# Two stacked transformer blocks on one core: the odd attention's probabilities scaled on GpSimd, the second turned tile taken by VectorE one step behind

## What is computed

```python
def window_attention(q, k, v, k_c, v_c, sink):       # 16 query heads, 4 key heads of 64
    s_loc = jnp.einsum('bkgnqd,bkncd->bkgnqc', qb, kb) * scale      # latent keys, |i-j| <= 128
    s_loc = jnp.where(valid, s_loc, -jnp.inf)
    s_ctx = jnp.einsum('bkgnqd,bkld->bkgnql', qb, k_c) * scale      # 256 context keys
    m = jnp.maximum(jnp.maximum(jnp.max(s_loc, -1, keepdims=True), jnp.max(s_ctx, -1, keepdims=True)), s_sink)
    e_loc = jnp.exp(s_loc - m)
    e_ctx = jnp.exp(s_ctx - m)
    denom = jnp.sum(e_loc, -1, keepdims=True) + jnp.sum(e_ctx, -1, keepdims=True) + jnp.exp(s_sink - m)
    o = (jnp.einsum('bkgnqc,bkncd->bkgnqd', e_loc, vb)
         + jnp.einsum('bkgnqc,bkld->bkgnqd', e_ctx, v_c)) / denom
```

## Time and profile before

| | |
|---|---|
| time, median of 3 runs | 2239.7 us (2237.48 to 2242.08) |
| the profiled execution | 2240.83 us, its span 2239.0 us |
| busy in the span | PE 97%, DVE 80%, ACT 53%, POOL 5% |
| odd attention in the span | about 1946 to 2006 us |
| TensorE's granted clock, mean | 0.992 of full speed |

### The profile page before, as it was taken

How to read it: one execution, slowest core, us unless ns; L and a number is a source line. 1 busy time by engine, 2 the same in 40 slices (tenths; PEclk the granted TensorE clock), 3 DMA queues, 4 the chain that set the end, 5 groups by cost and what they waited for, 6 DMA issues and landing times.

```text
span 2239.0 us, 34046 instructions
## 1 busy us (share of the span) xinstructions
PE 2162.9 (97%) x14088; PEld 1885.2 (84%) x14088; DVE 1796.2 (80%) x2404; ACT 1184.7 (53%) x1785; POOL 109.9 (5%) x157
## 2 busy tenths in 40 slices
PE   7999999999999999999999999999999999999997
PEld 4888889888878889898888978878888888767886
DVE  4988787788888878878888777779798988787764
ACT  3554556555455445655544545437646744485742
POOL 1000000000000000000000000000000000000000
PEclk9999999999999999999999999999999999999999
DMA  9889665488858868556887717528778877404662
GB/s 333 283 278 325 220 221 197 151 268 278 300 194 278 303 209 294 174 186 209 277 309 243 263 27 246 202 68 290 266 279 268 298 260 254 132 5 153 218 209 76
DMA packets 330881, 506.28 MB, mean 226 GB/s; under 512 B 12375, under 2 KB 239926, under 8 KB 330727
## 3 DMA queue, kind: packets, MB, share of 16 engines
q1 hardware_dynamic: 288503, 341.75, 46.1%
q0 software_dynamic: 41616, 160.44, 20.6%
q10 hardware_dynamic: 608, 1.92, 0.3%
HBM read 503.03 MB, written 1.05 MB: 225 GB/s over the span
## 4 chain that ended last, share of the span: by engine, by line
PE 78%; DVE 14%; DMA 3%; ACT 3%; issue 1%; POOL 0%; DVEq 0%; ACTq 0%; POOLq 0%
PE banks L617 35%; PE banks L618 18%; PE banks L609 6%; PE banks L611 5%; PE banks L610 5%; DVE wlo L1874 3%; PE banks L801 1%; DMA plain_xs<-in_ada_w_dram 1%; DVE arena L1899 1%; PE banks L862 1%; DVE nraw L2146 1%; DMA modw<-in_w_mod_dram 1%; DMA stage<-in_ffn_wg_dram 1%; DVE plain_hs L1899 1%; DVE xs L2150 1%
## 5 line engine op out<-in xcount | busy, mean ns | idle before, releaser
L1874 DVE TENSOR_TENSOR wlo<-stage,whi 128x1024 fp32r<-128x1024 f32 x644 | 757.9, 1219 | 136.1 <-ACT whi L1378 135.0
L1378 ACT CAST whi<-stage 128x1024 fp32r<-128x1024 f32 x644 | 643.9, 1051 | 351.6 <-PE banks L618 265.7
L617 PE MATMUL banks<-xs,whi 128*128 128x512 f32 x2176 | 766.4, 397 | 15.0 <-DVE xs L2150 9.5
L618 PE MATMUL banks<-xs,wlo 128*128 128x256 f32 x2176 | 608.7, 280 | 0.0
L617 PEld LDWEIGHTS banks<-xs,whi 128*128 128x128 f32 x2176 | 408.8, 188 | 116.5 <-DVE xs L2150 9.4
L618 PEld LDWEIGHTS banks<-xs,wlo 128*128 128x128 f32 x2176 | 411.1, 189 | 0.0
L609 PE MATMUL banks<-xs,whi 128*128 128x256 f32 x1216 | 352.1, 290 | 15.0 <-DVE xs L2072 7.9
L617 PE MATMUL banks<-hidden_arena,whi 128*128 128x512 f32 x992 | 354.6, 399 | 0.2 <-DVE wlo L1874 0.2
L610 PE MATMUL banks<-xs,whi 128*128 128x256 f32 x1216 | 344.6, 283 | 0.0
L611 PE MATMUL banks<-xs,wlo 128*128 128x256 f32 x1216 | 344.5, 283 | 0.0
L618 PE MATMUL banks<-hidden_arena,wlo 128*128 128x256 f32 x992 | 278.8, 281 | 0.0
(11 more groups left out here) (414 smaller groups left out, 2716.8 us busy)
## 6 DMA issues: line engine op xcount, KB each, us to landing
stage<-in_mlp_w_dram SPq DMA_DIRECT2D x96, 1024.0 KB, 5.5
modw<-in_w_mod_dram POOLq DMA_DIRECT2D x80, 1024.0 KB, 5.9
modw<-in_ada_w_dram POOLq DMA_DIRECT2D x66, 1024.0 KB, 5.5
stage<-in_ffn_wg_dram SPq DMA_DIRECT2D x44, 1024.0 KB, 5.5
stage<-in_ffn_wu_dram SPq DMA_DIRECT2D x44, 1024.0 KB, 7.3
stage<-in_ffn_wd_dram SPq DMA_DIRECT2D x44, 1024.0 KB, 7.2
stage<-in_ev_w_in_dram SPq DMA_DIRECT2D x24, 1024.0 KB, 6.5
stage<-in_w_in_dram SPq DMA_DIRECT2D x18, 1024.0 KB, 5.3
```

The lines of the kernel that those rows point to most:

```text
L617: mm(out, hi, pair.rearrange("p a t -> p (a t)"), start=first_mm, stop=False, skip_group_check=True)
L618: return mm(out[:, 0:T], lo, pair[:, 0, :], start=False, stop=last_mm, skip_group_check=True)
L1378: nc.scalar.copy(halves(whi[:, s, :], n, h, True), halves(stage[:, s, :], n, h)).then_inc(hi_done, 1)
L1874: last = v.tensor_tensor(halves(wlo[:, s, :], n, h, True), halves(stage[:, s, :], n, h), halves(whi[:, s, :], n, h, True).bitcast(F32), AL ...
```

## The change

DVE's `normalise(s)` stops after the reciprocal and signals `odshare` with a small memset. POOL scales the two tiles, all 16 steps of it ahead of the last modulation vector's transfers in its queue, and PE's `turn(s)` waits for POOL. ACT's `take(s)` copies the first turned tile only. DVE copies the second in `take_second(s-1)`, behind `normalise(s)`. The waits follow: `exps(s)` for the turn of step s-2, the reciprocal for POOL's step s-2 (its column is reused), `values(s)` and `turn(s)` for both takers.

```diff
+        pool_out = signal("pool_out")
...
+            def normalise(s):
+                o = 20 * (s % 2)
+                pool.wait_ge(dve_out.sem, dve_out.at(("odshare", s)))
+                for e in range(2):
+                    p = ODD["p"][s % 2][:, e, :]
+                    last = nc.gpsimd.tensor_scalar(p, p, stat[:, o + 12 + e:o + 13 + e], None, ALU.mult)
+                last.then_inc(pool_out.sem, pool_out.next(("odprob", s)))
             for m in range(NMOD):
+                if m == NMOD - 1:
+                    for s in range(16):
+                        normalise(s)
...
                 def turn(s):
-                    pe.wait_ge(dve_out.sem, dve_out.at(("odprob", s)))
+                    pe.wait_ge(pool_out.sem, pool_out.at(("odprob", s)))
                     for e in range(2):
                         if s >= 1:
-                            pe.wait_ge(drained.sem, drained.at(("odpt", s - 1, e)))
+                            taker = drained_v if e else drained
+                            pe.wait_ge(taker.sem, taker.at(("odpt", s - 1, e)))
...
                 def values(s):
-                    pe.wait_ge(drained.sem, drained.at(("odpt", s, 1)))
+                    pe.wait_ge(drained.sem, drained.at(("odpt", s, 0)))
+                    pe.wait_ge(drained_v.sem, drained_v.at(("odpt", s, 1)))
...
                 def exps(s):
+                    if s >= 2:
+                        act.wait_ge(pe_out.sem, pe_out.at(("odpt", s - 2, 1)))
...
                 def take(s):
-                    for e in range(2):
-                        act.wait_ge(pe_out.sem, pe_out.at(("odpt", s, e)))
-                        if s >= 2 and e == 0:
-                            act.wait_ge(pe_out.sem, pe_out.at(("odpv", s - 2)))
-                        nc.scalar.copy(O["pt"][s % 2][:, :, e * P:(e + 1) * P], Y[:, 2 + e, :].rearrange("p (a q) -> p a q", a=4)) \
-                            .then_inc(drained.sem, drained.next(("odpt", s, e)))
+                    act.wait_ge(pe_out.sem, pe_out.at(("odpt", s, 0)))
+                    if s >= 2:
+                        act.wait_ge(pe_out.sem, pe_out.at(("odpv", s - 2)))
+                    nc.scalar.copy(O["pt"][s % 2][:, :, 0:P], Y[:, 2, :].rearrange("p (a q) -> p a q", a=4)) \
+                        .then_inc(drained.sem, drained.next(("odpt", s, 0)))
...
                     link(v.tensor_tensor(stat[:, o + 10:o + 12], stat[:, o + 6:o + 8], stat[:, o + 8:o + 10], ALU.add))
+                    if s >= 2:
+                        dve.wait_ge(pool_out.sem, pool_out.at(("odprob", s - 2)))
                     link(v.reciprocal(stat[:, o + 12:o + 14], stat[:, o + 10:o + 12]))
-                    for e in range(2):
-                        last = v.tensor_scalar(O["p"][s % 2][:, e, :], O["p"][s % 2][:, e, :], stat[:, o + 12 + e:o + 13 + e], None, ALU.mult)
-                    done(last, ("odprob", s))
+                    done(v.memset(stat[:, 64:65], 0.0), ("odshare", s))
+
+                def take_second(s):
+                    dve.wait_ge(pe_out.sem, pe_out.at(("odpt", s, 1)))
+                    if s >= 2:
+                        dve.wait_ge(pe_out.sem, pe_out.at(("odpv", s - 2)))
+                    v.tensor_copy(O["pt"][s % 2][:, :, P:2 * P], Y[:, 3, :].rearrange("p (a q) -> p a q", a=4)) \
+                        .then_inc(drained_v.sem, drained_v.next(("odpt", s, 1)))
...
                     normalise(s)
+                    if s >= 1:
+                        take_second(s - 1)
                     if s == 0:
                         rotate(5)
+                take_second(15)
```

## The result

The changed kernel takes 2269.45 us in the median (2263.14 to 2271.3, 4 runs), the kernel before 2240.89 beside it (2237.48 to 2244.7). The ratio is 1.0122, 95% interval 1.0096 to 1.0149. By the medians it is 28.6 us slower, where 7 were forecast; the end of the range, 2256, lies 15 above the kernel before.

The account below looks back on a forecast made before the run. The bound was taken to be the odd attention's PE-DVE-PE loop, 3.18 us a step, with PE nearly saturated at 3.11. Loop +5.9 and ramp +1.1 gave +7.0 on the median 2239.7: 2246.7 us, range 2241 to 2256.

Parts of the forecast that it names:

- The loop: Odd attention, PE to DVE to PE: 6.35 us a two-step pass, 7.34 with POOL; six passes cost +5.9 us.
- 8u - 5: Forecast change of the kernel's time in us, by POOL's time for a pair of tiles; +7.0 in the forecast.
- u: POOL's time to scale one step's two tiles, taken as 1.5 us, between 0.88 and 2.44.
- the way from DVE to POOL: Delay in each pass from DVE's memset to POOL's start, taken as 0.30 us.
- The ramp: Start of the odd attention: turn(2) would start at 1963.71 instead of 1962.63, +1.1 us.
- The two tiles on POOL: POOL's scaling in each pass of the loop, the unknown term: 1.5 us, upper bound 2.44.
- the rival of the clock: Rival: longer gaps drop PE's clock to 1.2 GHz for the stage, +19 us, about 2266; chance 0.03.
- the slow POOL: Rival: POOL's pair takes 2.0 to 2.44 us and more, +11 to +15, time 2251 to 2255; chance 0.18.
- the copy on DVE: DVE's new copy of the second turned tile, 0.68 us a step, done while DVE would wait: no cost.
- ACT's relief: ACT gives up one copy of 0.59 us a step but is not on the loop: gain 0.
- POOL's queue: The last vector's transfers go out after step 15, near 2011, with 40 us of slack: no cost.
- Contention: Rival: DVE and POOL block each other beside rotate(5), 0 to 1 us once; counted inside the forecast, no own chance.

Follow-up runs that it names:

- e8: Changed kernel with POOL scaling only the first 256 of 512 columns of each tile, the rest unscaled: 2249.34 us against 2241.64 for the kernel before, ratio 1.0037.
- e9: Changed kernel with POOL's scaling written as a product with a repeated column: 2251.48 us against 2240.63 for the kernel before, ratio 1.0046.
- e4: Changed kernel plus ten idle matmuls on zeros a step while PE waits for POOL: 2260.08 us against 2239.91 for the kernel before, ratio 1.0090.
- e2: Changed kernel with only the scaling moved to POOL; ACT copies both turned tiles: 2268.83 us, ratio 1.0130 to the kernel before.
- e1: Changed kernel with only the second tile's copy moved to DVE; DVE still scales both tiles: 2247.28 us against 2239.91 for the kernel before, ratio 1.0033.
- e3: Changed kernel with DVE scaling the first tile and POOL only the second: 2244.07 us, ratio 1.0017 to the kernel before.
- e6: Kernel before plus 20 unrelated POOL operations on free blocks beside the attention, two transfers moved behind them: 2245.62 us against 2241.64, ratio 1.0024.
- e7: Changed kernel with a third probabilities buffer, the turn one step later, and POOL scaling only the second tile, DVE the first: 2243.01 us, ratio 1.0006 to the kernel before.
- e5: Changed kernel with a third probabilities buffer and turn, copies and values one step later: 2243.22 us against 2241.64 for the kernel before, ratio 1.0008.
- e10: Changed kernel with a third buffer, the turn one step later, and POOL's scaling as a product: 2239.50 us against 2240.63 for the kernel before, ratio 0.9995.

## Why the prediction was wrong

**The loop: right.** Chain, order and number of passes are those of the prediction. Its formula 8u - 5 is near where the clock holds in the attention: with u = 1.83 it gives +9.6 (e8: +7.7), with 2.05 it gives +11.4 (e9: +10.9), with 3.11 it gives +19.9 (e4: +20.2). One part is 0.2 us too high a pass, the way from DVE to POOL. I took it from a transfer's start, 0.30; for arithmetic it is 0.09. Over the eight passages that is 1.7 us, so the fit within half a microsecond in e9 and e4 is in part luck: in e4 the fillers on the chain stand against it, in e9 the lower clock behind the attention.

**The ramp: right.** Its sum is 2u - 1.92, for two passages through POOL. With u = 3.11 that is +4.3; the profile has +4.40.

**The step that failed: "The two tiles on POOL".** The term was mis-sized, 1.5 for a measured 3.11 us. It is worth 8 x 1.61 = 12.9 us, and with it alone the forecast, 2259.6, would lie beyond the range. My upper bound, 2.44, took POOL for an engine of half DVE's ordinary rate, which no row showed; tensor_scalar runs below that. The rows held no POOL arithmetic, so this bound should have been wide open, or the form of the instruction should have been part of the question: on POOL a copy, a product and tensor_scalar of one shape take 0.62, 1.10 and 1.56 us. The GPSIMD Engine Reference of the Trainium skill (Performance versus the Vector engine) has 4497 ns for a two-input add of 2048 columns; a quarter of it, 1.12 us, is an estimate for 512. The runs agree for tensor_tensor, with 1.02 to 1.10. The same page (Engine selection) calls one-input operations roughly line-rate. For the copy that is not far off: 0.62 us, where DVE took 0.68 and 0.75 for 512 columns at its ordinary rate. For tensor_scalar with 1.56 us the measurement decides against it.

**The second failure: the rival of the clock.** I gave it 0.03, as a clock at 1.2 GHz throughout for 19 us, and argued with gaps of 0.5 us. With u = 3.11 they are 2 us and more. The clock fell for part of each pass, 0.83 in the mean. In the profiles the six passes lose 60.44 - 6 x 8.76 = 7.9 us by it. The 1.6 us between turn(14) and the projection are the clock's as well: turn(14) takes 1.97 us instead of 1.09 and the values behind it 1.66 instead of 1.02. So are the 1.5 us behind the attention: in e4, which sends the two transfers as late as the change does, the stretches from 2030 on are at 1.00, and the way from the projection to the end takes 230.5 us. Together these are 11.0 of the 29.8 us between the spans; by the medians of e4 and the change the clock is worth 8.4. The other 18.8 us are the loop and its ramp. Its condition depended on u, and I did not carry it into the case of the slow POOL. Slow POOL and fallen clock were one case, not two.

**Nothing for the copy on DVE, ACT's relief and POOL's queue: right.** e2 shows the first. The two transfers went out at 2030.44, and the next one follows its place of before by 2094.79 - 2065.04 = 29.75 us, the shift of all that stands behind the attention. What the prediction left unsaid is that the copy alone costs 7 us (e1), where DVE still scales. So the change consists of a loss and of a second loss that the first one covers.

**Contention: right to leave it out of the steady state.** POOL's tiles took 1.56 us throughout, except one of the first pair with 1.82, beside rotate(5); that is 0.3 us, within the 0 to 1 that the rival allowed. Where DVE scales beside POOL, one of them gets longer: POOL's tile in e3 (1.74 for 1.56), DVE's pair in e6. The page SBUF — State Buffer of the Trainium skill (SBUF: two separate sides) describes this as a lock on the pair of ports that the two share, in which the later one waits for the whole instruction of the other. DVE's pairs with 1.70 and 2.27 for 0.88 us, beside POOL's copy, sum and product of 0.6 to 1.1, fit it; no run tests the lock by itself.

**Open.** How the lengths of the gaps make the clock fall was not measured. With passes of 7.5 to 7.7 us it stays at 1.00 for most of the stage (e8, e9), with 8.8 and no fillers it falls; between them no run was made. Behind the attention the gaps cannot be the whole cause: in e1, e7, e8 and e9 the clock was 1.00 through most of the attention and still 0.66 to 0.87 in a stretch at the start of the projection, and in the kernel before, e3, e4, e5, e6 and e10 it was not.

## What to carry to other kernels

Three engines at 90% and more do not show which one has room; the chain of waits does, and it said that the scaling stood in a loop of latencies where any engine slower than DVE is paid for on every pass. To move work to an idle engine, first take it out of the short loop (a third buffer and a turn one step later was worth 27 of 28.6 us), and count what that leaves: here the floor of PE, 1 us away. Where a longer wait opens gaps on PE, price the clock in the same case as the wait.

## What the runs showed of the hardware

- On POOL tensor_scalar on 128x512 float32 takes 1.56 us, a product with a repeated column 1.02 to 1.10, a copy 0.62, a memset 0.52; tensor_scalar on 256 columns takes 0.92 to 1.01.
- DVE's tensor_scalar pair took up to 2.27 us instead of 0.88 beside unrelated POOL operations, and the kernel was 4 us slower with 20 of these (and two transfers moved) in it.
- PE idle for 2 us and more once a pass had its granted clock at 0.83 in the mean; idle matmuls in these gaps held it at 1.00 and made the kernel 8.4 us faster.
